# Hybrid decoder step on one core: a later wait into the out product, the second norm and the last rows turned later, results turned inside the last down stage

## The reference, cut to what matters

```python
mixed = jax.nn.sigmoid(gate_a) * y_a + jax.nn.sigmoid(gate_b) * y_b
x = x + mixed @ w_out

h = _rmsnorm(x, norm_ffn_w).astype(x.dtype)
u, new_ffn_conv = _causal_dwconv(h @ w_up, ffn_conv_buf, ffn_conv_w)
u_gate, u_val = jnp.split(u, 2, axis=-1)
x = x + (jax.nn.silu(u_gate) * u_val) @ w_down
return x, (new_gdn_conv, new_gdn_S, new_C, new_n, new_m, new_ffn_conv)
...
y_prompt = _rmsnorm(yp, norm_final_w).astype(x_prompt.dtype)
y_sample = _rmsnorm(ys, norm_final_w).astype(x_sample.dtype)
```

## Time and profile before

| | |
|---|---|
| median of 3 runs (lowest to highest) | 1997.52 us (1996.8 to 1998.51) |
| the profiled execution's own time | 1997.32 us |
| its span in the profile | 1995.6 us |
| mean granted clock of TensorE over the span | 0.991 |
| PE / DVE / ACT / POOL busy | 98% / 61% / 46% / 10% |
| DMA | 308.14 MB, mean 154 GB/s |

### The profile page before, as it was taken

How to read it: one execution, slowest core, us unless ns; L and a number is a source line. 1 busy time by engine, 2 the same in 40 slices (tenths; PEclk the granted TensorE clock), 3 DMA queues, 4 the chain that set the end, 5 groups by cost and what they waited for, 6 DMA issues and landing times.

```text
span 1995.6 us, 39057 instructions
## 1 busy us (share of the span) xinstructions
PE 1945.9 (98%) x14362; PEld 1889.1 (95%) x14362; DVE 1218.3 (61%) x2506; ACT 917.3 (46%) x1785; POOL 193.3 (10%) x318
## 2 busy tenths in 40 slices
PE   9899999999999999999999999999999999999997
PEld 8799999999999999999999999999999999999996
DVE  5656666666655556556655577664576764466743
ACT  5444444454444444445544444443445443344533
POOL 2111221112100101100012100000000000000032
PEclk9899999999999999999999999999999999999999
DMA  8445555554556566555676466656666655656551
GB/s 215 122 120 144 142 142 135 139 145 129 146 134 177 147 173 169 151 155 163 181 188 164 129 170 169 166 153 168 172 162 159 167 155 164 172 150 169 158 149 64
DMA packets 572456, 308.14 MB, mean 154 GB/s; under 512 B 10639, under 2 KB 566823, under 8 KB 572343
## 3 DMA queue, kind: packets, MB, share of 16 engines
q1 hardware_dynamic: 530515, 279.14, 51.9%
q10 hardware_dynamic: 41828, 27.49, 4.7%
HBM read 293.58 MB, written 13.02 MB: 154 GB/s over the span
## 4 chain that ended last, share of the span: by engine, by line
PE 87%; DVE 4%; ACT 3%; issue 3%; SPq 1%; ACTq 1%; POOL 1%; DMA 0%; DVEq 0%; POOLq 0%
PE products L1718 26%; PE products L1720 25%; PE products L1719 25%; PE mixer L1699 2%; DVE w_lo L556 1%; ACT w_hi L549 1%; PE mixer L1827 1%; PE mixer L1833 1%; PE mixer L1942 1%; PE products L1873 1%; PE mixer L1781 0%; PE products L1898 0%; PE products L1699 0%; ACT conv_out L891 0%; DVE u_val L1634 0%
## 5 line engine op out<-in xcount | busy, mean ns | idle before, releaser
L556 DVE TENSOR_TENSOR w_lo<-w_raw,w_hi 128x512 fp32r<-128x512 f32 x1037 | 721.6, 709 | 681.9 <-ACT w_hi L549 679.1
L549 ACT ACTIVATE w_hi<-w_raw 128x512 fp32r<-128x512 f32 x1037 | 632.1, 627 | 666.6 <-PE products L1720 644.1
L1718 PE MATMUL products<-h_hi,w_hi 128*128 128x288 f32 x1536 | 479.9, 312 | 1.6 <-DVE w_lo L556 1.5
L1719 PE MATMUL products<-h_lo,w_hi 128*128 128x288 f32 x1536 | 456.8, 297 | 0.0
L1720 PE MATMUL products<-h_hi,w_lo 128*128 128x288 f32 x1536 | 456.4, 297 | 0.0
L1718 PE MATMUL products<-f_hi,w_hi 128*128 128x288 f32 x1408 | 417.8, 297 | 1.0 <-ACT r L1109 1.0
L1720 PE MATMUL products<-f_hi,w_lo 128*128 128x288 f32 x1408 | 417.3, 296 | 0.0
L1719 PE MATMUL products<-f_lo,w_hi 128*128 128x288 f32 x1408 | 414.1, 294 | 0.0
L1718 PEld LDWEIGHTS products<-h_hi,w_hi 128*128 128x128 f32 x1536 | 292.2, 190 | 16.4 <-issue 10.1
L1719 PEld LDWEIGHTS products<-h_lo,w_hi 128*128 128x128 f32 x1536 | 291.5, 190 | 0.6
L1720 PEld LDWEIGHTS products<-h_hi,w_lo 128*128 128x128 f32 x1536 | 290.2, 189 | 0.0
(11 more groups left out here) (426 smaller groups left out, 2296.4 us busy)
## 6 DMA issues: line engine op xcount, KB each, us to landing
w_raw<-in_w_in SPq DMA_DIRECT2D x95, 1024.0 KB, 6.0
w_raw<-in_w_up SPq DMA_DIRECT2D x88, 1024.0 KB, 5.8
w_raw<-in_w_down SPq DMA_DIRECT2D x32, 1024.0 KB, 5.8
w_raw<-in_w_out SPq DMA_DIRECT2D x16, 1024.0 KB, 7.4
w_raw<-in_w_down SPq DMA_DIRECT2D x16, 768.0 KB, 4.9
w_raw<-in_w_branch_a SPq DMA_DIRECT2D x8, 1024.0 KB, 5.2
w_raw<-in_w_branch_b SPq DMA_DIRECT2D x8, 1024.0 KB, 5.3
S_sample<-in_state_gdn_S ACTq DMA_DIRECT2D x8, 512.0 KB, 7.9
```

Of the source, the lines that this page charges most:

```text
L549: nc.scalar.activation(ring_slot(whi, whi2, n, ring), raw[:, s % slots, 4 * j:4 * j + 4], ACT.Copy).then_inc(hi_ready, 1)
L556: nc.vector.tensor_tensor(ring_slot(wlo, wlo2, n, ring), raw[:, s % slots, 4 * j:4 * j + 4], ring_slot(whi, whi2, n, ring).bitcast(F32), A ...
L1718: mm(out, w_hi, x_hi, start=start, stop=False)
L1719: mm(out, w_hi, x_lo, start=False, stop=False)
```

## The change

- Into the out product: PE waits for the mix tiles of three passes only; the wait for the fourth goes to the last block of each column tile. The turns of x go from behind block 0 to ahead of it, in each of the four groups. The sample rows come in as four tiles of 32 rows on 128 partitions (`xg4`), so that one turn serves four tiles: nine turns per group in place of twelve. ScalarE copies them in one more step, `xs`.
- Second norm: the FFN's first block waits for three quarters of `f_lo`; the wait for the last quarter goes to the last block of a column tile. The sum over `ssq` is done after block 1 of the first gate group, and the wait for the logarithm comes after the first round, which is written out ahead of the loop.
- Last rows: their turn moves from behind block 0 to behind block 7 of a down group (block 5 in the last stage).
- Results: in the last down stage ScalarE weights a tile by the norm's weight as soon as its sum is done (`weigh`), PE turns it one block later (`turn_y`), and ScalarE copies it to `y_rows` (`rows`). That is done for 15 of the 16 tiles. rstd is then applied per token on the finished rows, by VectorE and ScalarE a half row at a time, and SP issues five stores. POOL adds up the squares of 15 tiles, and ScalarE squares the last one. The sums become columns (`SUMS`), begun ahead of the last block. The table load for the logarithm goes ahead of the last down groups.

```diff
-            pe.wait_ge(*br_d.before(4))
+            pe.wait_ge(*br_d.before(3))
             pe.wait_ge(*no_a.after("p"))
 
             def turn_input(i):
                 pe.wait_ge(x_in2, 32 * i + 32)
                 pe.wait_ge(*ot_a.before(i))
+                turn(pm[:, 3, T:T + P], xg4[:], P).then_inc(*ot_t.done("xs"))
                 for m in range(4):
-                    for n, t0, c in PARTS:
-                        last = turn(pm[:, m, t0:t0 + n], xg[0:n, c, m * P:(m + 1) * P], n)
+                    for n, t0, c in PARTS[:2]:
+                        last = turn(pm[:, m, t0:t0 + n], xg[:, c, m * P:(m + 1) * P], n)
                     last.then_inc(*ot_t.done(f"x{m}"))
-                yield 0
 
             with pe.Fori(0, 4) as i:
-                pe_group(i + q_out, i + g_out, mix_hi, mix_lo, turn_input(i), 16, ring=8)
+                turn_input(i)
+                pe_group(i + q_out, i + g_out, mix_hi, mix_lo, ring=8, x_last=br_d.before(4))
...
             last.then_inc(*n2_t.done("w"))
-            pe.wait_ge(*ot_p.before(4))
-            mm(pm[:, 0, 0:T], ones[:], ssq[:], start=True, stop=True).then_inc(*n2_t.done("sum"))
-            pe.wait_ge(*ot_d.before(4))
-            pe.wait_ge(*n2_d.after("w"))
-            pe.wait_ge(*n2_a.after("ln"))
+            pe.wait_ge(*ot_d.before(3))
+            def norm_sum():
+                yield 0
+                pe.wait_ge(*ot_p.before(4))
+                pe.wait_ge(*n2_d.after("w"))
+                mm(pm[:, 0, 0:T], ones[:], ssq[:], start=True, stop=True).then_inc(*n2_t.done("sum"))
+                yield 0
...
+                if c == 0:
+                    up(0, itertools.chain(norm_sum(), old_rows(g0)), ot_d.before(4))
+                    pe.wait_ge(*n2_a.after("ln"))
+                with pe.Fori(0, n - (c == 0)) as i:
+                    k = i + (c == 0)
+                    up(k, old_rows(k + g0))
...
                 def last_rows(r):
+                    for _ in range(2 * n - 1):
+                        yield 0
                     pe.wait_ge(*dn_p.after("sel", r))
                     pe.wait_ge(*dn_a.before(r))
                     turn(pm[:, 0, 0:P], u_out[:], P).then_inc(*dn_t.done("tr"))
                     yield 0
...
+                    def turn_y(t):
+                        if t < KT - 1:
+                            pe.wait_ge(*y_a.after(f"ws{t}"))
+                        else:
+                            pe.wait_ge(*y_d.after("ws15"))
+                        if t >= 2:
+                            pe.wait_ge(*y_a.after(f"r{t - 2}"))
+                        if t >= 5 and t % 4 in (1, 2):
+                            pe.wait_ge(*y_a.after(f"rs{t // 4 - 1}"))
+                        bank = pm[:, 2 + t % 2]
+                        for h in range(2):
+                            last = turn(bank[:, h * P:(h + 1) * P], yt[:, t % 4, h * P:(h + 1) * P], P)
+                        if t % 4 == 3:
+                            last = turn(bank[:, TP:TP + P], yts[:].rearrange("p m t -> p (m t)"), P)
+                        last.then_inc(*y_t.done(f"t{t}"))
+                    SUMS = [(pm[:, 0, 0:1], slice(0, P)), (pm[:, 1, 0:1], slice(P, TP)), (ps[:, 0, 0:1], None)]
+                    def visits(i):
+                        rows = last_rows(4 * c + i) if i < n else last_rows_p()
+                        for b in range(4 * n):
+                            if b % n == 1 and 4 * i + b // n > 0:
+                                turn_y(4 * i + b // n - 1)
+                            if b == n + 2:
+                                for _ in rows:
+                                    pass
+                            if i == 3 and b == 4 * n - 2:
+                                pe.wait_ge(*fin_p.after("s4"))
+                                pe.wait_ge(*dn_a.before(11))
+                                pe.wait_ge(*pl_a.after("r"))
+                                for out, cc in SUMS:
+                                    mm(out, ssq[:, cc] if cc else ssq4[:], ones[:, 0:1], start=True, stop=False)
+                            yield 0
                     for i in range(4):
-                        pe_group(q, g + i, u_hi, u_lo, last_rows(4 * c + i) if i < n else last_rows_p(), 16,
-                                 ring=8, b0=4 * n * i, n=n, x_last=x_last)
+                        pe_group(q, g + i, u_hi, u_lo, visits(i), 4 * n, ring=8, b0=4 * n * i, n=n, x_last=x_last)
+                    pe.wait_ge(*y_a.after("q"))
+                    for out, cc in SUMS[:2]:
+                        last = mm(out, sq_l[:, cc], ones[:, 0:1], start=False, stop=True)
+                    last.then_inc(*y_t.done("sum"))
+                    pe.wait_ge(*y_a.after("qs"))
+                    mm(SUMS[2][0], sq_l4[:], ones[:, 0:1], start=False, stop=True).then_inc(*y_t.done("sums"))
+                    turn_y(KT - 1)
```

On ScalarE, in the last down stage and behind it:

```diff
+                    def weigh(t):
+                        act.wait_ge(*freed(g + 2 * n + t // 4, t % 4))
+                        if t >= 4:
+                            act.wait_ge(*y_t.after(f"t{t // 4 * 4 - 1}"))
+                        nc.scalar.activation(yt[:, t % 4, 0:TP], x2[:, t, 0:TP], ACT.Copy, scale=wn[:, 2, t:t + 1]).then_inc(*y_a.done(f"w{t}"))
+                        nc.scalar.activation(yts[:, t % 4], x2[:, t, TP:T], ACT.Copy, scale=wn[:, 2, t:t + 1]).then_inc(*y_a.done(f"ws{t}"))
+                        if t:
+                            rows(t - 1)
+                    def rows(t):
+                        act.wait_ge(*y_t.after(f"t{t}"))
+                        nc.scalar.activation(y_rows[:, :, t * P:(t + 1) * P], pm[:, 2 + t % 2, 0:TP].rearrange("p (c n) -> p c n", c=2),
+                                             ACT.Copy).then_inc(*y_a.done(f"r{t}"))
+                        if t % 4 == 3:
+                            nc.scalar.activation(ys_rows[:, t // 4], pm[:, 2 + t % 2, TP:TP + P], ACT.Copy).then_inc(*y_a.done(f"rs{t // 4}"))
...
+                        points = [(n * m + n - 1, lambda t=4 * i + m: weigh(t)) for m in range(4) if 4 * i + m < KT - 1]
+                        if i == 3:
+                            points.append((4 * n - 3, lambda: rows(KT - 2)))
...
+            act.wait_ge(*freed(g - 1, 3))
+            nc.scalar.activation(sq_l[:], x2[:, KT - 1], ACT.Square).then_inc(*y_a.done("q"))
+            nc.scalar.activation(in_four(sq_l4[:]), fourfold(x2[:, KT - 1, TP:T]), ACT.Square).then_inc(*y_a.done("qs"))
...
+                nc.scalar.activation(y_rows[:, 1, cc], y_rows[:, 1, cc], ACT.Copy, scale=rs[:, 1:2]).then_inc(*y_a.done(f"s1{half}"))
```

More of the change, by code:

```diff
@@ L1 @@
+import itertools
 import concourse.bass as bass
@@ L522, in _ @@
             sp.wait_ge(lrow_out, 16 * N_LROW)
-            sp.wait_ge(y_out, 16 * 8)
+            sp.wait_ge(y_out, 16 * 5)
         TAIL = CHUNKS[-1]
@@ new lines, in _ @@
+            act.wait_ge(*freed(g - 1, 3))
+            nc.scalar.activation(sq_l[:], x2[:, KT - 1], ACT.Square).then_inc(*y_a.done("q"))
+            nc.scalar.activation(in_four(sq_l4[:]), fourfold(x2[:, KT - 1, TP:T]), ACT.Square).then_inc(*y_a.done("qs"))
+            for name, src, to, ready in (("", pm[:, 0:2, 0:1].rearrange("p c n -> p (c n)"), rs[:, 0:2], "sum"), ("s", ps[:, 0, 0:1], rs[:, 2:3], "sums")):
+                act.wait_ge(*y_t.after(ready))
+                nc.scalar.activation(to, src, ACT.Ln, bias=eps[:], scale=1.0 / D).then_inc(*y_a.done("ln" + name))
+                act.wait_ge(*y_a.after("ln" + name))
+                nc.scalar.activation(to, to, ACT.Exp, scale=-0.5).then_inc(*y_a.done("exp" + name))
@@ L1188, in _ @@
+            for half in range(2):
+                cc = slice(half * D // 2, (half + 1) * D // 2)
+                act.wait_ge(*y_a.after("exp"))
+                if half:
+                    act.wait_ge(*y_d.after("r15"))
+                nc.scalar.activation(y_rows[:, 1, cc], y_rows[:, 1, cc], ACT.Copy, scale=rs[:, 1:2]).then_inc(*y_a.done(f"s1{half}"))
         @block.vector
@@ L2076, in _ @@
                 else:
-                    for i in range(4):
-                        pe_group(q, g + i, u_hi, u_lo, last_rows(4 * c + i) if i < n else last_rows_p(), 16,
-                                 ring=8, b0=4 * n * i, n=n, x_last=x_last)
-                q, g = q + n, g + 4
-            pe.wait_ge(*fin_p.before(KT))
-            mm(pm[:, 3, 0:T], ones[:], ssq[:], start=True, stop=True).then_inc(*y_t.done("sum"))
-            pe.wait_ge(*dn_a.before(11))
-            pe.wait_ge(*pl_a.after("r"))
```

105 lines of the change are left out of this document (54 added, 51 removed).

## The result

The changed kernel takes 1981.66 us (median of four runs, 1980.09 to 1983.73), the kernel before 1997.67 in the same comparison (1996.8 to 1998.51). The ratio is 0.9922, 95% interval 0.991 to 0.9934: 16.0 us faster, where 19.0 were forecast. The time lies 3.4 us above the forecast of 1978.3, inside the range and inside the likeliest case's own bounds.

What follows compares the result with a forecast made beforehand. TensorE, busy 1945.9 of 1995.6 us, was taken as the bound, so only holes in its stream and the tail could be won. 5.9 - 2.4 + 4.8 + 6.4 - 3.5 + 7.8 = 19.0 us gave 1978.3, range 1971 to 1989.

Steps and rivals of the forecast that it cites:

- the likeliest case: The forecast itself, all its terms holding: 1978.3 us, given 66%, by its own bounds 1973 to 1984.
- Into the out product and its groups: Out product: 5.9 us won by starting block 1 earlier, 2.4 lost to uncovered f_hi waits in the three other groups.
- Second norm: Between out product and FFN: first FFN block earlier and clock kept, 4.8 us won, bounds 2.2 to 5.3.
- PE does not run dry: FFN start: seven blocks split ahead, 11 us, cover the later sum and the ScalarE and VectorE work queued behind it.
- Last rows: Down stages: turn moved later avoids PE's waits for POOL's copy, 6.4 us won, bounds 4.5 to 7.
- The rival by which holes only move: Blocks freed from mix_lo, norm and copy wait for splits queued behind the same VectorE work; 1995.4 us, chance 5%.
- Turns in the stream: Last down stage: 33 turns of results between its blocks cost 3.5 us in all.
- the stall ahead of the last block: Before the last block PE waits for ScalarE's copies, then does three one-column sums: 1.8 us lost, bounds 1 to 2.5.
- the rival on the other side: Last down stage: weighted tiles come late, PE loses time at fifteen tiles; time passes 2001 us, chance 6%.
- The tail: After the last product: 21.6 us shrink to 12.0; less 1.8 lost ahead of the last block, 7.8 won.
- The rival of slow stores: Tail: one queue carries all stores at 149 GB/s, 15.8 us, 9 less gain; 1987.4 us, chance 7%.
- the rival of the out groups alone: Clock falls behind the three out-group holes if turns do not keep it up; 1983.1 us, chance 4%.

Runs made afterwards that it cites:

- E9: Changed kernel with the wait for all mix tiles and the turns behind block 0 as before, but nine turns per group; 1984.03 us, ratio 0.9931.
- E2: Changed kernel with the turns of x and of the convolution weights waiting only for the copies they overwrite, group loop written out; 1976.51 us, ratio 0.9901.
- E3: Changed kernel with the second norm's sum after block 0 of the first gate group, not after block 1; 1981.68 us, ratio 0.9924.
- E8: Changed kernel with the second norm as before: sum, logarithm and all of f_lo ahead of the FFN; 1983.91 us, ratio 0.9938.
- E4: Changed kernel with the turn of the last rows back behind block 0 in the first two down stages; 1984.9 us, ratio 0.9939.
- the second profile: Profile of the changed kernel run once more, unaltered; that run measured 1982.2 us, ratio 0.9923.
- E1: Changed kernel with the sample rows stored as four stores of 32 rows in place of one; 1978.44 us, ratio 0.991.
- E6: Changed kernel with E2's and E3's edits and the sample rows in four stores, two each by SP and ScalarE; 1971.14 us, ratio 0.9863.
- E7: Changed kernel with 16 extra matmuls into an unread bank in the u_lo holes of down stages one and two; 1980.5 us, ratio 0.9912.
- E10: E6 with ten and sixteen extra matmuls filling the u_lo holes of the first and second down stage; 1970.21 us, ratio 0.9869.

## Why the prediction came out as it did

**Into the out product and its groups: right in sum, off in its parts.** Forecast 5.9 - 2.4 = 3.5, measured 5.25. Block 1 comes 2.5 us after the branch products' end, 9.0 before, a gain of 6.5; nine turns took 0.90, not 1.4, which is the term that was mis-sized. The holes in the other groups are three, at 1.44 apiece, as named; their loss is 0.41 each and not 0.8 (group period 28.30 us against 27.88), since nine turns (0.95 us, from 1020.58 to 1021.53) replace twelve of 2.24. E9 and E2 show that the early turns are worth 0.6 as built and some 5 more with the narrower wait in the out groups alone.

**Second norm: right, with a price that the forecast put at nothing.** Forecast 4.8, measured 4.9. But "PE does not run dry" looked only at the splits ahead of PE. ScalarE's and VectorE's work on the first products starts later behind PE too, and that delay is carried through all four rounds to u_lo: E3 gives 1.3 us of it back by a sum one block earlier, and so does E8 with the norm as before (holes of 1.57 and 1.62 in place of 2.90). E8 finds the part to be worth 2 to 3. The 0.5 for the sum in the stream stood without a row; it measured 0.47.

**Last rows: the failed step.** It took the u_lo times of the earlier trace rows as if they would come forward with PE, and so forecast holes of some 1.5 and 1.9 us; they are 2.90 and 2.23 of waiting. In stage one the norm's edit had put u_lo 1.25 us further behind PE. The rival by which holes only move named waits for the weight splits, and none of those appears; but a hole did move, to u_lo. The 0.9 of stage one is there when the sum is earlier (E3); as built, stage one lost 2.1 us in one profile (clock fallen) and 0.6 in the other, and stage two won 0.2 and 1.65 of the forecast 2.1. E4 shows that the turn's new place is still worth some 1.2 us at the same clock and about 3 in the median. In stage three the two waits of 1.75 are gone, as forecast.

**Turns in the stream and the stall ahead of the last block: right.** No wait for a weighted tile appears, so the rival on the other side fell. Rest and ten blocks of stage three lost 1.7 against 1.9. In the stall, the last block starts 1.87 us after the turns of tile 14 (forecast 1.8 and 0.2 for the turns).

**The tail: the other mis-sized term,** 6.5 won where 9.6 were forecast (21.6 to 12.0). The chain up to the stores ran a little faster than forecast: the first is asked for 3.2 us after the last product, at 3.5 in the forecast. Its terms without a row, the sum at 0.75 and the two functions at 0.3 each, measured 0.64, 0.26 and 0.20. The missing 3.1 us is the sample rows' store. The forecast set the finer *load* of those rows at nothing, rightly, and let their *store* run in the rate of all 2.36 MB. The rival of slow stores named one shared queue as the cause and the sum as the price; E1 shows that it was the shape of one store.

**The clock.** In the profile of after it did not fall behind the f_hi holes or the turns of any out group, nor behind the weight turns (1.00 in the windows that begin at 1020.58, 1048.80, 1077.00 and 1105.57), so the rival of the out groups alone fell. The Trainium skill's "TensorE: Matmul & The Clock Gate", section "Part 4: PE-mode transpose", says that transposes do not count as PE-busy in the same way. The rows here do not bear that out. If turns did not count, the 2.55 us between the products of two out groups (1018.98 to 1021.53, hole and nine turns) would be a longer stretch without work than the u_lo holes of stage two, of 2.06 to 2.33 us (2.2 to 2.5 from product to product), which brought a fall in seven of nine profiles; yet at none of 21 such out group starts, in seven profiles, did the clock fall.

Behind the u_lo holes of stage one it fell in four of six profiles with 2.90 to 3.01 us, and in none of three with 1.57 to 1.62 (E3, E6, E8). A fall cost 1.45, close to the 1.6 forecast. What decides it between two executions with nearly the same hole stays open; E7 and E10 only show that with the holes filled it did not fall in the one profile of each. The trace of before held a sign of this that the prediction passed over: of the two waits of 2.4 us in the earlier trace rows it read the second, and behind the first the clock was 1.00 (1325.60 to 1329.00).

The three errors stand against each other: 1.75 too little in the out product, 4.9 too much in the first two down stages (2.0 in the second profile), 3.1 too much in the tail. That the time came within 3.4 us of the forecast is in part luck.

## What to carry to other kernels

When a wait is moved later, follow the engine behind the one that gains: VectorE's last result must come forward by as much as TensorE does, or the hole only stands at the next stage's end. Wait for the steps whose data are overwritten, not for a whole round of steps. When a layout is changed so that a load or a turn becomes cheaper, price the store of the new shape by itself, above all if it is the last one.

## What the runs showed of the hardware

A store of 256 KB with an outer dimension of four ran at 28 to 88 GB/s, where 512 KB stores on 128 partitions ran at 385 to 418; cut into four of 32 rows, the tail was 3.1 us shorter. Turns behind a hole of 1.44 us did not let the granted clock fall (none of 21 places), and a hole of 3.01 us left it at 1.00 in one profile while one of 2.90 brought 0.51 in another. A fall cost the stream of products 1.45 us.
